# The expert stage of a hybrid encoder layer: weights as the moving operand, split into fp32r parts

## The reference, cut to what matters

```python
def expert_block(args):
    xblk, e = args
    hdn = jax.nn.silu(xblk @ w_gate_e[e]) * (xblk @ w_up_e[e])
    return hdn @ w_down_e[e]
```

## Time and profile before

| what | us |
|---|---|
| median of 3 runs | 2809.85 |
| the profiled execution | 2812.55 |
| its span, first to last instruction | 2811.0 |
| last stage before the experts ends, x of block 0 asked for | 2048.5 |
| first gate matmul | 2054.6 |
| last store of the expert stage issued | 2763.0 |
| one block of the expert stage | 22.0 |

### The profile page before, as it was taken

The page is one execution under the profiler, slowest core; times in us unless marked ns, Lnnn a source line. Parts: engine busy times, 40 slices in busy tenths (PEclk is TensorE's granted clock), DMA queues, the critical chain, the costliest instruction groups (busy, mean ns, idle before and its releaser), DMA issues. The chain is left out here.

```text
span 2811.0 us, 38540 instructions
## 1 busy us (share of the span) xinstructions
PE 2419.6 (86%) x14272; PEld 1997.4 (71%) x14272; DVE 888.5 (32%) x1415; ACT 640.4 (23%) x1073; POOL 168.7 (6%) x175
## 2 busy tenths in 40 slices
PE   4678979888797988899999599899279999999992
PEld 3566867667686766899888499845168877888772
DVE  5345354544535453211456432111400000000003
ACT  3133232332322221211465331111000101101010
POOL 0111010110101000000111100000200000000002
PEclk9888999999999975899999899999589999999996
DMA  3211120202111010310555431150568888888875
GB/s 90 59 39 32 46 77 0 77 1 77 31 46 55 0 55 4 121 45 28 150 177 165 139 103 45 52 193 0 187 217 327 309 318 326 326 327 314 313 291 201
DMA packets 237268, 376.83 MB, mean 134 GB/s; under 512 B 17840, under 2 KB 125656, under 8 KB 237176
## 3 DMA queue, kind: packets, MB, share of 16 engines
q1 hardware_dynamic: 216008, 302.26, 31.6%
q0 software_dynamic: 17600, 61.18, 6.8%
q10 hardware_dynamic: 3584, 12.58, 1.1%
HBM read 301.60 MB, written 74.39 MB: 134 GB/s over the span
## 5 line engine op out<-in xcount | busy, mean ns | idle before, releaser
L1715 PEld LDWEIGHTS e_gate_ps<-e_xT,e_gate 128*128 128x128 f32 x2048 | 236.0, 194 | 17.1 <-issue 17.1
L1715 PE MATMUL e_gate_ps<-e_xT,e_gate 128*128 128x96 f32 x2048 | 235.5, 276 | 1.1 <-DVE e_xT L1752 1.1
L1715 PE MATMUL e_up_ps<-e_xT,e_up 128*128 128x96 f32 x2048 | 233.9, 275 | 0.0
L1715 PEld LDWEIGHTS e_up_ps<-e_xT,e_up 128*128 128x128 f32 x2048 | 231.3, 192 | 0.0
L1726 PE MATMUL e_y_ps<-e_down,e_hT 128*96 128x512 f32 x512 | 227.4, 597 | 0.0
L1763 DVE TENSOR_TENSOR e_hT<-e_act,e_up_ps 128x384 f32<-128x384 f32 x32 | 17.7, 553 | 649.4 <-PE e_up_ps L1715 649.4
L1252 DVE COPY probsT<-turn_ps 128x512 f32<-128x512 f32 (+4 forms) x232 | 131.5, 567 | 249.0 <-PE turn_ps L1022 225.0
L101 PE MATMUL proj_ps<-w_qkv_hi,xh 128*128 128x384 f32 x544 | 194.3, 357 | 9.3 <-PEq L285 9.3
L1042 PEld LDWEIGHTS out_ps<-v_new,probsT 128*128 128x128 f32 x1152 | 156.9, 207 | 61.5 <-DVEq L84 45.0
L1152 ACT ACTIVATE probs_s<-scores,neg_max 128x256 f32<-128x256 f32 (+7 forms) x128 | 95.1, 743 | 445.6 <-DVEq L84 445.1
L1042 PE MATMUL out_ps<-v_new,probsT 128*128 128x64 f32 x1152 | 177.1, 294 | 21.2 <-DVEq L84 20.2
(11 more groups left out here) (344 smaller groups left out, 4093.2 us busy)
## 6 DMA issues: line engine op xcount, KB each, us to landing
e_gate<-w_gate_e SPq DMA_DIRECT2D x32, 2048.0 KB, 9.3
e_up<-w_up_e SPq DMA_DIRECT2D x32, 2048.0 KB, 15.1
e_down<-w_down_e SPq DMA_DIRECT2D x32, 2048.0 KB, 13.5
slot_x<-zrows POOLq DMA_DIRECT2D x48, 440.0 KB, 6.4
e_x<-slot_x SPq DMA_DIRECT2D x33, 384.0 KB, 13.0
w_qkv<-w_in SPq DMA_DIRECT2D x24, 512.0 KB, 9.8
slot_y<-e_y ACTq DMA_DIRECT2D x32, 384.0 KB, 6.1
slot_y<-zrows POOLq DMA_DIRECT2D x24, 352.0 KB, 9.6
```

The lines of the kernel that those rows point to most:

```text
L1715: last = te.matmul(out[:, f * CAP:(f + 1) * CAP], weights[u][:, k, f * P:(f + 1) * P], xT[:, k, :], start=(k == 0), stop=(k == KT - 1))
```

## The change

**The product.** All three products of a block now have the tokens stationary (96 columns) and the weights moving, 512 columns at a time, in fp32r parts: per block 8 gate, 8 up and 8 down products of three matmuls each, 72 matmuls. The hidden values come out with the tokens on the partitions, so `turn_h` turns them (4 transposes) before the down product.

**The parts.** The weights come in six pieces of 1.05 MB (128 partitions by 2048): 0 and 1 gate, 2 and 3 up, 4 and 5 down. There is one raw buffer per piece, and no second set. ACT casts a piece to its hi part and DVE subtracts for its lo part; the parts live in a ring of three buffers, and a piece is cast only when the piece three before it in the order has been used by PE. x and the turned hidden values are split in the same way.

**The order.** PE does the gate and up products of block b+1 (`inner`), turns x of block b+2, and then does the down product of block b (`outer`). So the order in which pieces are split is 0, 1, 2, 3 of block b+1 and then 4, 5 of block b. The loop is over single blocks.

**The loads.** In its pass i, SyncE loads pieces 0 to 3 of block i+1, x of block i+2, then pieces 4 and 5 of block i+1. Each piece waits until the piece that was in its raw buffer has been split. All six pieces of block 0 are loaded in `merge`; nothing is loaded in `route`. A row of a piece is 4 KB in HBM (before: 2 KB for gate and up, 4 KB for down).

Besides, the semaphores of the first two stages are given back and cleared by SyncE early in `attend`.

```diff
     def load(self, sp, g, c, e):
+        half = slice(c % 2 * 2, c % 2 * 2 + 2)
+        if c < 4:
+            w = (g.w_gate_e, g.w_up_e)[c // 2]
+            src = w[0, bass.ds(e, 1)].rearrange("o (a p b) n -> p (o a) (b n)", p=P, b=2)[:, half, :]
+        else:
+            src = g.w_down_e[0, bass.ds(e, 1)].rearrange("o (a p) n -> p (o a) n", p=P)[:, half, :]
+        sp.dma_start(self.raw[c][:, :].rearrange("p (a n) -> p a n", a=2), src).then_inc(self.loaded[c], 16)
...
             @block.sync
-                with sp.Fori(0, n - 1) as i:
-                    for u in range(2):
-                        b = i * 2 + u
-                        e = sp.value_load(expert_of[0:1, bass.ds(b + 2, 1)], min_val=0, max_val=EXPERTS - 1)
-                        sp.wait_ge(x_turned, b + 2)
-                        load_x(b + 2, u)
-                        sp.wait_ge(up_ready, b + 1)
-                        w.load_in(sp, g, u, e)
-                        sp.wait_ge(y_ready, b + 1)
-                        w.load_down(sp, g, u, e)
+                with sp.Fori(0, n * 2 - 1) as i:
+                    e = sp.value_load(expert_of[0:1, bass.ds(i + 1, 1)], min_val=0, max_val=EXPERTS - 1)
+                    for c in range(PIECES):
+                        if c == 4:
+                            sp.wait_ge(x_turned, i + 2)
+                            alone(sp, g)
+                            load_x(i + 2)
+                        split = i * PIECES + (c + 1 if c < 4 else c + 1 + PIECES)
+                        sp.wait_ge(wh_ready, split)
+                        sp.wait_ge(wl_ready, split)
+                        alone(sp, g)
+                        w.load(sp, g, c, e)
...
             @block.tensor
+                def piece(c, u, at):
+                    pe.wait_ge(wh_ready, at + 1)
+                    pe.wait_ge(wl_ready, at + 1)
+                    alone(pe, g)
+                    for r in range(4):
...
+                        last = product(nc, out, parts, (w_hi[u][:, cols], w_lo[u][:, cols]), k == 0, k == last_k)
+                    last.then_inc(w_used, 1)
+                def inner(b, later):
...
+                    piece(0, 0, b * PIECES)
+                    if later:
+                        turn_h(b - 1)
+                    piece(1, 1, b * PIECES + 1)
+                    piece(2, 2, b * PIECES + 2)
+                    piece(3, 0, b * PIECES + 3)
...
+                with pe.Fori(0, n * 2 - 1) as i:
+                    inner(i + 1, True)
+                    turn_x(i + 2)
+                    outer(i, 1, i * PIECES + PIECES + 4)
...
             @block.scalar
+                def high(c, u, b, at, ringed=True):
+                    act.wait_ge(w.loaded[c], b * 16 + 16)
+                    if ringed:
+                        act.wait_ge(w_used, at + 1)
+                    alone(act, g)
+                    sc.copy(w_hi[u][:, :], w.raw[c][:, :]).then_inc(wh_ready, 1)
...
+                def step(b, later):
+                    at = b * PIECES
+                    high(0, 0, b, at)
+                    high(1, 1, b, at + 1)
+                    high(2, 2, b, at + 2)
+                    if later:
+                        keep_y(b - 2, at)
+                    high_h(b - 1)
+                    high(3, 0, b, at + 3)
+                    silu(b)
+                    if later:
+                        store_y(b - 2)
+                    high(4, 1, b - 1, at + 4)
+                    high(5, 2, b - 1, at + 5)
+                    high_x(b + 1)
...
             @block.vector
+                with dve.Fori(0, n * 2 - 1) as i:
+                    at = i * PIECES + PIECES
+                    low(0, 0, at)
+                    low(1, 1, at + 1)
+                    low(2, 2, at + 2)
+                    low_h(i)
+                    low(3, 0, at + 3)
+                    low(4, 1, at + 4)
+                    low(5, 2, at + 5)
+                    hidden(i + 1)
+                    low_x(i + 2)
```

More of the change, by code:

```diff
@@ L878, in _ @@
                 load_past_k(0)
+                for done in g.early:
+                    sp.sem_clear(done)
                 store_kv(0)
@@ L1613, in _, with load @@
                 chain(v.tensor_copy(expert_of[:, :], table_f[:, :]))
+PIECES, PIECE, RING = 6, 2048, 3
 class ExpertWeights:
     def __init__(self, nc, g, ctx):
[L1621 to L1641, removed]
+        self.raw = [ctx.enter_context(nc.sbuf_tensor(f"e_raw{c}", [P, PIECE], F32)) for c in range(PIECES)]
+        self.loaded = [g.sem(f"e_loaded{c}") for c in range(PIECES)]
+    def load(self, sp, g, c, e):
+        half = slice(c % 2 * 2, c % 2 * 2 + 2)
[5 more added lines that the diff above has]
+        sp.dma_start(self.raw[c][:, :].rearrange("p (a n) -> p a n", a=2), src).then_inc(self.loaded[c], 16)
 def experts(nc, g, w, passes, expert_of):
@@ L1745, in _, with high_x @@
-                for u in range(2):
-                    act.wait_ge(y_stored[u], n * 16 + 16)
+                sc = nc.scalar
+                def high(c, u, b, at, ringed=True):
[4 more added lines that the diff above has]
+                    sc.copy(w_hi[u][:, :], w.raw[c][:, :]).then_inc(wh_ready, 1)
+                def high_x(b):
+                    act.wait_ge(x_turned, b + 1)
+                    sc.copy(x_view(x_hi), xT_ps[:, :, 0:4 * CAP]).then_inc(xh_ready, 1)
@@ new lines, in _ @@
+                n = act.value_load(passes[0:1, 0:1], **limits)
+                act.sem_inc(y_stored, 32)
+                high_x(0)
+                for c in range(3):
+                    high(c, c, 0, c, ringed=False)
+                high(3, 0, 0, 3)
+                silu(0)
+                high_x(1)
+                act.wait_ge(wh_ready, 4)
+                act.sem_inc(wh_ready, 2)
+                step(1, False)
+                with act.Fori(0, n * 2 - 2) as i:
+                    step(i + 2, True)
@@ L1750, in _ @@
             def _(dve):
[L1751 to L1765 removed]
+                v = nc.vector
@@ new lines, in _ @@
+                low_x(0)
+                for c in range(3):
+                    low(c, c, c, ringed=False)
+                low(3, 0, 3)
+                hidden(0)
+                low_x(1)
+                dve.wait_ge(wl_ready, 4)
+                dve.sem_inc(wl_ready, 2)
+                with dve.Fori(0, n * 2 - 1) as i:
[9 more added lines that the diff above has]
+                    low_x(i + 2)
@@ L1851, in layer, with early_sem @@
     g.sem = lambda name: ctx.enter_context(nc.semaphore(name))
+    g.early, early = [], ExitStack()
+    def early_sem(name):
+        g.early.append(early.enter_context(nc.semaphore(name)))
+        return g.early[-1]
+    g.early_sem = early_sem
     g.slots_cleared = g.sem("slots_cleared")
```

185 lines of the change are left out of this document (107 added, 78 removed).

## The result

The changed kernel takes 3029.12 us (median of 4 runs, 3022.99 to 3034.09); beside it the kernel before took 2810.53. The ratio is 1.077, with a 95% interval of [1.075, 1.080]: slower by 219 us. The forecast was 3030, +220. One execution of the kernel before among those beside the first experiments took 3738 us and one of ten of refill_fp32 took 5388; ratios, and the time given for refill_fp32, are of the others.

The account below looks back on a forecast made before the run. TensorE, busy all 200 us, was taken to bound the kernel before. After: 30 steps of 29.2 us (876) and 2110.4 for the rest end at 2986.4 against 2766.0, +220 on 2809.85, so 3030 us; 8 in 10 range 2955 to 3120.

Parts of the forecast that it names:

- What bounded before, and the parts: Expert stage: TensorE bound at 22.0 us a block; new matmuls and turning 17.9, casts 1.9 and subtractions 2.3 each.
- The queue runs dry once per block: SyncE's in-order queue waits for the split of piece 4, with nothing but x in flight; block 29.2 us.
- Transfers: Loads of six pieces, issue of piece 4 to landing of piece 3: 15.7 us of data plus 3.1 around it, 18.8.
- d: Time from the landing of piece 3 to the issue of piece 4, through TensorE, casts and subtraction: 10.4 us.
- faster transfers: Rival on the loads: fixed part 1.9 us and 408 GB/s, 27.7 us a block, 2985 us; chance 0.13.
- the two times by the page: Load times by the skill's figures: 2.0 us plus bytes over 436 GB/s gives 2958 us, 358 GB/s gives 3087.
- A: Experiments' theory from the forecast: queue dry once per block, all bytes from issue of piece 4 to landing of piece 3 count.
- Start and end: Outside the 30 steps: first landing of piece 3 at 2073.5, block 0 6.6 us late, 30.3 after the last; 2110.4.
- a full clock: Rival on TensorE's clock: it stays full, piece 0 ends sooner, 26.9 us a block, 2961 us; chance 0.11.
- a half clock: Rival on TensorE's clock: it never comes back in a burst, 33.1 us a block, 3147 us; chance 0.08.
- x between the pieces: Load of x ahead of the down pieces fills dry time; elsewhere it would add 1 us a block, 30 us.
- The queue that stays full: Rival on SyncE: it passes its wait for piece 4 with pieces in flight, 17.9 us a block, 2691; chance 0.03.

Follow-up runs that it names:

- refill_fp32: Against refill: no parts, 24 plain fp32 matmuls per block straight from the raw pieces, each buffer refilled once TensorE has used it; 2816.73 us, ratio 1.001.
- refill: Against the changed kernel: SyncE issues loads in the order in which the splits free the buffers, nothing else changed; 2741.39 us, ratio 0.974.
- half_123: Against the changed kernel: only the first half of pieces 1, 2 and 3 loaded in the loop, 4, 5 and 0 whole; 3030.69 us, ratio 1.077.
- warm: Against the changed kernel: 40 resultless matmuls on TensorE after piece 5 of each block, to hold the clock up; 2982.21 us, ratio 1.061.

## Why the prediction was right, and where it was not

- **What bounded before, and the parts.** Right. Matmuls of 512 columns start 0.23 and 0.42 us apart, a piece is 2.8 or up to 5.2 us, casts and subtractions 1.9 and 2.3. That the engines' own work would fit in some 18 us was borne out by refill, whose second to sixth blocks took 17.8 to 17.9 us.
- **The queue runs dry once per block.** Right, and shown by refill: 288 us hang on the order of the loads.
- **Transfers, 18.8 us from the issue of piece 4 to the landing of piece 3.** Right: 18.9 on the mean of the 30 blocks, 17.7 to 20.1 (19.4 in the block shown). 3.1 us around the data was chosen between two unlike loads, without a row for it, so that it came out so near is in part luck. The Trainium skill ("DMA: Bandwidth & Descriptors", "Anatomy of one DMA — SWDGE (gpsimd) path") gives about 2.0 us and the bytes over 436 GB/s, an estimate of 16.4 for the six pieces; no block of this trace, with its loads issued from SyncE, was under 17.7, so the time by that figure (2958) fell with it.
- **d, from that landing to the next issue of piece 4, 10.4.** Measured 28.87 - 18.89 = 10.0 on the mean. Piece 0 took 4.7 us on TensorE (4.1 to 5.2) where 5.3 was taken for every block; its split took 0.3 more than was taken.
- **The path itself.** The circle is right and its name is wrong. In the forecast's own sum piece 0 lands at T - 7.9, and d follows from it by its split, TensorE, the turning of h, piece 1 and the silu: that is the measured circle, term for term, as the table shows. But the text starts the chain "at T, the landing of piece 3", for which the cast of piece 3 is said to wait, and no row above has that wait. What follows from this reading is wrong: the rival of faster transfers, and the two times by the page, hold d fixed and let all six pieces count, and the expectations of A do the same. half_123 decides it. With d fixed it would have been 118 us faster (3 x 1.31 x 30), and it is not faster at all. So the forecast is right for these bytes, and a change of the bytes would have been priced at up to twice its worth.
- **The block.** 29.2 forecast, 28.87 measured, 10 us too many over 30 steps. **Start and end.** x asked for to first issue of piece 4: 42.0 forecast (2073.5 + 6.6 + 10.4 - 2048.5), 42.7 measured. From the last issue of piece 4 to the last store: 16.9 forecast (27.3 - 10.4), 22.8 measured. The last down pieces too run at half clock, for 5.6 us (matmuls 0.43 us apart up to 2970.06), and TensorE could begin with piece 4 only when VectorE had subtracted piece 5, since the low part of h stands behind that (idle 5.89 us, ended by L1848 at 2964.43). These two misses nearly cancel.
- **The profiled execution.** Its last store is issued at 2974.28, 211.3 us later than in the earlier trace rows. The expert stage began 5.7 us earlier in it, which lies within the earlier stages' own spread (refill, whose earlier stages are the same code, asks for x at 2054.4, the kernel after at 2042.8), so the stage itself is 217 us longer, against 220.
- **Faster transfers, a full clock, a half clock.** None came. For the clock 2.3 us a block was taken (29.2 - 26.9); warm gave back 1.6, and 1.9 is the estimate for a clock that never falls. The rest is the same 5.1 us for every block again.
- **x between the pieces.** Called 1 us a block at most. The bytes are worth 1.0 us, as said; the place is worth 0.5, since moving x also frees piece 0 of the half clock (2.0) and keeps TensorE in the down product when piece 0 is split (1.5).
- **The queue that stays full, 2691.** Its mechanism was refill's. Its price was too low: 17.9 us a block for TensorE and 17.7 for the DMA engines at 0.4 MB/us, where refill has 19.3 on the mean. The first of these was met until the loads fell behind; the second was not, for 19.3 us are 7.08 MB at 367 GB/s, with the DMA share at 1.02. The transfers end the waits there, but slower than in the best windows of the earlier trace rows.

Left open: why a full queue moves 364 to 370 GB/s on the mean and 410 to 422 in single windows. Two windows of 2 us of the kernel refill show both, the second about the y store and the load of x:

```profile
2301.00:2303.00 2.00, 2.00 (x13) 1.70 (x14) 1.58 (x1) 1.05 (x2) 0.00 (x0) 1.00 1.03 422
...
2313.00:2315.00 2.00, 2.00 (x10) 1.39 (x9) 1.68 (x3) 1.50 (x2) 0.00 (x0) 1.00 1.04 248
```

The engines are as busy and move less. Whether x or y are what does it was not tried. Nor was a ring of four parts, which would take the cast of piece 3 from behind piece 0.

## What to carry to other kernels

When loads are issued by one in-order queue, issue them in the order in which their buffers come free, not in the order in which they are used: one load that waits for the wrong thing holds back all behind it, and here that was 288 us with the same work on every engine. When all engines are partly idle, write the circle of waits of one round with its times and check by experiment which landings lie in it, for a sum can come out right while the path is read wrong, and the next change is then priced wrong. A cheaper product (77 us here) shows only where its operands arrive in time.

## What the runs showed of the hardware that was not expected

- GpSimd's subtraction of 128 by 2048 fp32 takes 4.55 us, twice VectorE's 2.29, and while it runs a small two-input instruction on VectorE takes 3.5 to 4.3 us in place of 0.2 to 0.5. The Trainium skill ("SBUF — State Buffer", "Who interferes with whom") has the rule that VectorE instructions with two inputs in SBUF and GpSimd instructions that read it exclude each other for a whole instruction; the rows above agree, the one-input reduction at 0.19 us too.
- After idle times of 8.4 and 9.2 us in neighbouring blocks the clock came back 5.2 and 2.7 us into the burst. Over the 30 blocks, those with a mean clock of 0.88 took 27.4 to 28.1 us, those with 0.82 or 0.83 28.2 to 30.6. In warm it fell too, less than 1 us into the burst that came after only 2.3 us of idle time (block from 2306.87), and stayed at 1.00 after 2.1 us in the next.
- The store of y lands 3.0 us after its issue in the dry time, against 6.1 at the median before and 6.8 in refill: the time to landing tells here how full the queue is rather than how long the transfer takes.
- With the queue full the DMA share reads 1.02 at 364 GB/s in refill and 1.05 at 408 in the earlier trace rows: a full share is no fixed rate.
